# Products before the statistics: the first weight pair of three stages works on residual times channel scale

## The reference, cut to what matters

```python
def rms_norm(x, g):
    y = x32 * lax.rsqrt(jnp.mean(x32 * x32, axis=-1, keepdims=True) + RMS_EPS)
    return (y * g.astype(jnp.float32)).astype(x.dtype)
def modulate(h, shift, scale):
    return h * (1 + scale[:, None, :]) + shift[:, None, :]
...
    if layer == N_A_LAYERS:
        h_kv = modulate(rms_norm(x, kv_norm_g), kv_mod[:, 0], kv_mod[:, 1])
        kv_bands = shared_kv_bands(h_kv, kv_w, cos, sin)
    h = modulate(rms_norm(x, norm_g[layer, 0]), mod[:, 0, 0], mod[:, 0, 1])
    x = x + 0.5 * mod[:, 0, 2][:, None, :] * swiglu(h, ...)
    h = modulate(rms_norm(x, norm_g[layer, 1]), mod[:, 1, 0], mod[:, 1, 1])
    y = moba_mixer(h, ...) if layer < N_A_LAYERS else dilated_mixer(h, ...)
    x = x + mod[:, 1, 2][:, None, :] * y
    h = modulate(rms_norm(x, norm_g[layer, 2]), mod[:, 2, 0], mod[:, 2, 1])
    x = x + 0.5 * mod[:, 2, 2][:, None, :] * swiglu(h, ...)
```

## Time and profile before

| | us |
|---|---|
| median of 3 runs | 2489.45 |
| lowest, highest | 2488.74, 2490.04 |
| the profiled execution | 2490.71 |
| its span, first to last instruction | 2489.0 |
| mean granted TensorE clock | 0.997 |

### The profile page before, as it was taken

The page is one execution under the profiler, slowest core; times in us unless marked ns, Lnnn a source line. Parts: engine busy times, 40 slices in busy tenths (PEclk is TensorE's granted clock), DMA queues, the critical chain, the costliest instruction groups (busy, mean ns, idle before and its releaser), DMA issues. The chain is left out here.

```text
span 2489.0 us, 33283 instructions
## 1 busy us (share of the span) xinstructions
PE 2443.6 (98%) x11977; PEld 2015.8 (81%) x11985; DVE 1356.8 (55%) x2066; ACT 854.8 (34%) x1204; POOL 137.2 (6%) x128
## 2 busy tenths in 40 slices
PE   9999999999999999999999999999999999999998
PEld 6888886888778888878888888886888887888886
DVE  7555445677675654355545555445667667433333
ACT  3222223445443332233333333223344444333221
POOL 0000000112000000011211000000111110000000
PEclk9999999999999999999999999999999999999999
DMA  6666532665446654335557656345888973223332
GB/s 244 191 193 190 169 118 91 205 194 182 140 151 196 186 182 134 105 123 193 183 188 250 189 183 199 125 125 133 248 222 220 238 219 102 85 93 100 99 95 84
DMA packets 135714, 408.76 MB, mean 164 GB/s; under 512 B 17089, under 2 KB 17473, under 8 KB 135617
## 3 DMA queue, kind: packets, MB, share of 16 engines
q1 hardware_dynamic: 122560, 357.16, 47.6%
q0 software_dynamic: 13056, 50.33, 5.7%
HBM read 353.95 MB, written 52.43 MB: 163 GB/s over the span
## 5 line engine op out<-in xcount | busy, mean ns | idle before, releaser
L325 DVE TENSOR_TENSOR w_lo<-w_raw,w_hi 128x1024 fp32r<-128x1024 f32 (+2 forms) x386 | 473.3, 1227 | 650.5 <-ACT w_hi L321 650.5
L330 PE MATMUL ps<-h_hi,w_hi 128*128 128x512 f32 x1856 | 738.0, 398 | 11.0 <-DVE h_lo L880 4.6
L332 PE MATMUL ps<-h_hi,w_lo 128*128 128x512 f32 x1856 | 725.4, 391 | 0.0
L331 PE MATMUL ps<-h_lo,w_hi 128*128 128x512 f32 x1856 | 724.4, 390 | 0.0
L321 ACT CAST w_hi<-w_raw 128x1024 fp32r<-128x1024 f32 (+2 forms) x388 | 395.9, 1020 | 802.9 <-PE ps L332 788.2
L330 PEld LDWEIGHTS ps<-h_hi,w_hi 128*128 128x128 f32 x1856 | 349.6, 188 | 91.5 <-DVE h_lo L880 10.9
L332 PEld LDWEIGHTS ps<-h_hi,w_lo 128*128 128x128 f32 x1856 | 349.0, 188 | 74.2
L331 PEld LDWEIGHTS ps<-h_lo,w_hi 128*128 128x128 f32 x1856 | 349.9, 189 | 65.8
L330 PE MATMUL ps<-act_hi,w_hi 128*128 128x512 f32 x704 | 275.5, 391 | 0.0
L332 PE MATMUL ps<-act_hi,w_lo 128*128 128x512 f32 x704 | 274.2, 389 | 0.0
L331 PE MATMUL ps<-act_lo,w_hi 128*128 128x512 f32 x704 | 274.0, 389 | 0.0
(11 more groups left out here) (137 smaller groups left out, 2772.2 us busy)
## 6 DMA issues: line engine op xcount, KB each, us to landing
w_raw<-gate_up SPq DMA_DIRECT2D x176, 512.0 KB, 3.7
ada_raw<-ada SPq DMA_DIRECT2D x144, 512.0 KB, 4.6
w_raw<-down SPq DMA_DIRECT2D x80, 512.0 KB, 3.6
w_raw<-kv_w SPq DMA_DIRECT2D x48, 512.0 KB, 3.6
w_raw<-mixa_w SPq DMA_DIRECT2D x34, 512.0 KB, 4.3
w_raw<-mixb_w SPq DMA_DIRECT2D x34, 512.0 KB, 5.7
kb<-rot_st POOLq DMA_DIRECT2D x12, 1024.0 KB, 5.0
k_hi<-kb SPq DMA_DIRECT2D x64, 192.0 KB, 5.1
```

The costliest lines, as they stand in the source:

```text
L325: eng.tensor_tensor(w_lo[:, slot, 0:n], w_raw[:, slot, 0:n], w_hi[:, slot, 0:n].bitcast(F32), ALU.subtract).then_inc(w_lo_done[slot], 2)
L330: nc.tensor.matmul(out_ap, l_hi, r_hi, start=start, stop=False, skip_group_check=skip)
L331: nc.tensor.matmul(out_ap, l_hi, r_lo, start=False, stop=False, skip_group_check=skip)
L332: return nc.tensor.matmul(out_ap, l_lo, r_hi, start=False, stop=stop, skip_group_check=skip)
```

## The change

At the borders into mixA, kv and mixB, `pe_late_pair` takes the place of `pe_stats` and of the first weight pair. It multiplies the weights by x times channel scale, without token factor and shift. For the result h = x·a·r + s, with r a factor of the token and s a shift of the channel, the product of weights W and h is r·(W(x·a)) + W·s. So the two result banks are multiplied by r (`late_scale`, to SBUF), and W·s is summed by two-column products (`shift`: s as high and low column, with the high and the low weights) and added in `late_read`, together with the cosine or sine factor. The zero products of these borders are gone. Rows 0 to 5 of x times a (`late_high` on ACT, `late_low` on DVE) are made in the down projection after each of its first three pairs, rows 6 and 7 behind root and diagonal. The normalised h is still made row by row and is used from the second pair on; two weight splits stand in its midst (`LATE_SPLIT`). The stored modulation block moves behind the first reads, in kv TensorE's value products wait for it. The third weight transfer goes ahead of the tables on SP. In mixB the second pair takes its two units in an interleaved order, with bank 3 for its second.

The diff, cut to its core:

```diff
+LATE = ("mixA", "kv", "mixB")
+LATE_SPLIT = {"mixA": {1: 2, 5: 3}, "kv": {1: 2, 5: 3}, "mixB": {1: 2, 4: 3}}
+LATE_ROWS = (6, 7)
...
+        def pe_late_pair(pe, name):
+            e, r, u0, p0 = LATE.index(name), ROUND[name], UNIT0[name], PAIR0[name]
+            def weights(w, k, j):
+                if name == "mixB":
+                    return w[:, j, k * P:(k + 1) * P]
+                return w[:, k // 4, k % 4 * PAIR + j * P:k % 4 * PAIR + (j + 1) * P]
+            def rows(ks, halves=(0, 1)):
+                for k in ks:
+                    pe.wait_ge(late_lo_done, KT * e + k + 1)
+                    for j in halves:
+                        mm = three_passes(ps[:, j, :], weights(w_hi, k, j), weights(w_lo, k, j),
+                                          h_hi[:, k, :], h_lo[:, k, :], k == 0, k == KT - 1)
+                    if 1 in halves:
+                        mm.then_inc(late_used, 1)
+            def shift(ks, halves=(0, 1)):
+                for j in halves:
+                    for k in ks:
+                        for w in (w_hi, w_lo):
+                            mm = nc.tensor.matmul(shift_ps[:, 2 * j:2 * j + 2], weights(w, k, j), shift_hl[:, k, :],
+                                                  start=j == 0 and k == 0 and w is w_hi,
+                                                  stop=k == KT - 1 and w is w_lo, skip_group_check=True)
+                mm.then_inc(unit_used, 1)
+            def sums():
+                pe.wait_ge(sum_done, 9 * r)
+                for t in range(TT):
+                    mm = nc.tensor.matmul(stat[:, t:t + 1], tmp[:, 2, t * P:(t + 1) * P], ones[:, 0:1],
+                                          start=True, stop=True)
+                mm.then_inc(stat_done, 1)
+            def spread():
+                pe.wait_ge(diag_done, r + 1)
+                nc.tensor.matmul(rb, ones[:], diag[:].rearrange("p t n -> p (t n)"),
+                                 start=True, stop=True).then_inc(rb_done, 1)
+            pe.wait_ge(w_lo_done[0], u0 + 2)
+            pe.wait_ge(pair_free, p0 + 1)
+            pe.wait_ge(shift_split, 2 * e + 2)
+            if name == "mixB":
+                rows(range(4), (0,))
+                sums()
+                rows((4, 5), (0,))
+                pe.wait_ge(w_lo_done[1], u0 + 2)
+                rows((0, 1), (1,))
+                spread()
+                rows((6, 7), (0,))
+                shift(range(KT), (0,))
+                rows(range(2, KT), (1,))
+                shift(range(KT), (1,))
+            else:
+                rows((0, 1))
+                sums()
+                rows((2, 3))
+                spread()
+                shift(range(4))
+                pe.wait_ge(w_lo_done[1], u0 + 2)
+                rows(range(4, KT))
+                shift(range(4, KT))
+            pe.sem_inc(shift_summed, 1)
...
-            pe.wait_ge(pair_free, p0 + 2)
-            with pe.Fori(0, G * NB // 2) as i:
-                pe_pair(pe, i * 8 + u0, i * 4 + p0 - 2, 0, FULL_KS, kv_h_hi, kv_h_lo, h_ready)
-                pe_pair(pe, i * 8 + u0 + 2, i * 4 + p0 - 1, 2, FULL_KS, kv_h_hi, kv_h_lo)
+            def values(i):
                 for j in range(4):
                     pe.wait_ge(w_lo_done[j % 2], i * 8 + u0 + 4 + j - j % 2 + 2)
                     if j == 0:
-                        pe.wait_ge(rb_kept_done, 1)
+                        pe.wait_ge(rb_kept_done, LATE.index("kv") + 1)
+                        pe.wait_ge(xar_done, KT * NORMS.index("ffn2"))
                         pe.wait_ge(pair_free, i * 4 + p0 + 2)
...
+            pe.wait_ge(pair_free, p0 + 2)
+            pe_pair(pe, u0 + 2, p0 - 1, 2, FULL_KS, kv_h_hi, kv_h_lo, h_ready)
+            pe.wait_ge(shift_done, LATE.index("kv") + 1)
+            pe.wait_ge(mod_ready, ADA_IN_FFN[1] + ADA_LOOPED + 1)
+            values(0)
+            with pe.Fori(1, G * NB // 2) as i:
+                pe_pair(pe, i * 8 + u0, i * 4 + p0 - 2, 0, FULL_KS, kv_h_hi, kv_h_lo)
+                pe_pair(pe, i * 8 + u0 + 2, i * 4 + p0 - 1, 2, FULL_KS, kv_h_hi, kv_h_lo)
+                values(i)
...
-                    for n in range(24):
+                    for n in range(KT, 2 * KT) if is_a else (8, 9, 12, 13, 10, 11, 14, 15):
                         substep(g, n)
+                    for n in range(2 * KT, 24):
+                        substep(g, n)
+                    pe.wait_ge(shift_done, LATE.index(name) + 1)
...
+        def late_cols(dve, name, block, gain_row, col_n):
+            e = LATE.index(name)
             dve.wait_ge(mod_ready, block + 2)
             nc.vector.scalar_tensor_tensor(out=a_col[:], in0=mod[:, block + 1, :], scalar=1.0,
                                            in1=gain[:, gain_row, :], op0=ALU.add,
                                            op1=ALU.mult).then_inc(col_ready, 1)
+            if e > 0:
+                dve.wait_ge(shift_summed, e)
+            nc.vector.tensor_copy(shift_hl[:, :, 0], mod[:, block, :]).then_inc(shift_split, 1)
+            dve.wait_ge(shift_split, 2 * e + 1)
+            nc.vector.tensor_tensor(shift_hl[:, :, 1], mod[:, block, :], shift_hl[:, :, 0].bitcast(F32),
+                                    ALU.subtract).then_inc(shift_split, 1)
+            dve.wait_ge(col_ready, col_n)
+        def late_high(act, name, n, col_n):
+            act.wait_ge(col_ready, col_n)
+            nc.scalar.activation(h_hi[:, n, :], x[:, n, :], ACT.Copy, scale=a_col[:, n:n + 1]).then_inc(late_hi_done, 1)
+        def late_low(dve, name, n):
+            dve.wait_ge(late_hi_done, KT * LATE.index(name) + n + 1)
+            nc.vector.scalar_tensor_tensor(out=h_lo[:, n, :], in0=x[:, n, :], scalar=a_col[:, n:n + 1],
+                                           in1=h_hi[:, n, :].bitcast(F32), op0=ALU.mult,
+                                           op1=ALU.subtract).then_inc(late_lo_done, 1)
+        def late_views(name):
+            if name == "kv":
+                return rb_kept[:], next_tmp[:]
+            return att[:, 0, :], att[:, 1:3, :]
+        def late_scale(dve, name):
+            e, (factor, scaled) = LATE.index(name), late_views(name)
+            dve.wait_ge(shift_summed, e + 1)
+            nc.vector.tensor_reduce(shift_out[:], shift_ps.rearrange("p (j h) -> p j h", j=2),
+                                    mybir.AxisListType.X, ALU.add).then_inc(shift_done, 1)
+            dve.wait_ge(unit_used, UNIT0[name] + 2)
+            dve.wait_ge(rb_kept_done, e + 1)
+            view = by_class if name == "mixA" else classes
+            for j in range(2):
+                nc.vector.tensor_tensor(view(scaled[:, j, :]), classes(ps[:, j, :]), classes(factor),
+                                        ALU.mult).then_inc(late_scaled, 1)
+            dve.wait_ge(late_scaled, 2 * e + 2)
+            dve.sem_inc(pair_free, 1)
+        def late_read(dve, name, rope_n, half):
+            e, scaled = LATE.index(name), late_views(name)[1]
+            if half == 0:
+                dve.wait_ge(shift_done, e + 1)
+                dve.wait_ge(rope_done, rope_n)
+            for n in (2 * half, 2 * half + 1):
+                src, table = ((0, cos), (1, sin), (1, cos), (0, sin))[n]
+                op = nc.vector.scalar_tensor_tensor(out=tmp[:, n, :], in0=scaled[:, src, :],
+                                                    scalar=shift_out[:, src:src + 1], in1=table[:],
+                                                    op0=ALU.add, op1=ALU.mult)
+            op.then_inc(late_rope, 1)
...
+                if name in LATE and k - 1 in LATE_SPLIT[name]:
+                    n = LATE_SPLIT[name][k - 1]
+                    w_split_lo(dve, UNIT0[name] + n, n % 2)
             low(KT - 1)
+            if name in LATE:
+                late_scale(dve, name)
...
+                if name in LATE and name != "kv":
+                    act.wait_ge(late_used, KT * LATE.index(name) + k + 1)
                 nc.scalar.activation(view(to_hi[:, k, :]), classes(tmp[:, 3 + k % 2, :]), ACT.Identity,
                                      bias=mod[:, block, k:k + 1]).then_inc(h_hi_done, 1)
+                if name in LATE and k in LATE_SPLIT[name]:
+                    n = LATE_SPLIT[name][k]
+                    w_split_hi(act, UNIT0[name] + n, n % 2)
+            if name in LATE:
+                act.wait_ge(xar_done, x0 + KT)
+                nc.scalar.copy(late_views(name)[0], rb).then_inc(rb_kept_done, 1)
+                w_split_hi(act, UNIT0[name] + 4, 0)
...
+                    if late is not None:
+                        for j in range(2):
+                            if i * 4 + 2 * b + j not in LATE_ROWS:
+                                late_high(act, late[0], i * 4 + 2 * b + j, late[1])
...
+                    w_split_lo(dve, u0 + 4, 0)
+                    mod_store(dve, ADA_IN_FFN[1] + ADA_LOOPED)
+                    for half in range(2):
+                        late_read(dve, "kv", 2 * n0, half)
+                    w_split_lo(dve, u0 + 5, 1)
```

(23 more changed lines are left out.)

146 lines of the change are left out of this document (90 added, 56 removed).

## The result

The changed kernel takes 2503.97 us (median of 4 runs, 2503.59 to 2507.19) where the kernel before, beside it, takes 2489.66. The ratio is 1.0061, 95% interval 1.0043 to 1.0078. It is **slower by 14 us**; 11 us faster was forecast. The profiled execution took 2503.81, span 2502.1 (before 2490.71 and 2489.0).

The account below looks back on a forecast made before the run. TensorE, busy for 98% of the span, was taken as the bound, with empty work at three borders. Gains 2.5 + 4.1 + 6.0 less 1.7 made 10.9 us: forecast 2478.5, range 2472 to 2485.

Parts of the forecast that it names:

- What is moved at no cost: Down projection and borders: late rows, norm rows, third weight transfer and POOL's additions were said to move without cost.
- 0.23: TensorE's pitch in us for a 512-column product in full flow, used to size the first pair's 48 products at 11.0.
- The slower rival: Late rows in the down projection push a split past its unit; nine pairs lose 2.8 each: 2503.8, chance 0.05.
- What would show it: Signs at the borders: first part 16.6, two-column products 0.115, mixA waits 2.4 and about 3, unit 7 six us earlier.
- kv, 4.1: Border into kv: second pair begins at 1088.8 instead of 1092.91, no wait behind it, gain 4.1 us.
- mixA, 2.5: Border into mixA: VectorE's chain to the keys limits the gain to 2.5 us, between 1 and 4.9.
- The wait before it: MixA, unit 4: TensorE waits 2.4 us for VectorE's weight split, done at 435.9.
- the 1.7 of the sum: One clock fall, expected from the 3.1 us idle before mixA's first score, costing 1.7 us.
- The clock's rival: The clock falls at the narrow sums too: 13.6 against 12.6, so 2490.4, no change; chance 0.09.
- mixB, 6.0: Border into mixB: unit 7's weight transfer comes 6 us earlier, gain 6.0 us, between 2.4 and 7.
- The first rival: The first queries' store may hold unit 7's transfer; mixB gives 2.4, 7.3 in all, 2482.1; chance 0.14.

Follow-up runs that it names:

- e7: The changed kernel with its idle tile 96 bytes shorter, so the streamed tiles stand where they stood in the kernel before: 2484.36 us, ratio 0.9979.
- e5: The changed kernel with unused columns in shift_out, so tiles behind it stand 256 bytes further on than in the kernel before: 2483.96 us, ratio 0.9978.
- e8: The changed kernel with tiles placed as in e7 and mixB's key load issued after unit 5, not right ahead of unit 7: 2480.38 us, ratio 0.9960.
- e12: The same kernel as e8 once more, over more rounds, beside the kernel before: 2481.53 us, ratio 0.9966.
- e4: The kernel before with act_lo alone moved by 32 bytes: 2501.12 us, ratio 1.0034.
- e2: The kernel before with an unused tile of 32 bytes per partition ahead of the tile idle: 2512.18 us, ratio 1.0090.
- e10: The kernel before with an unused tile of 32 bytes between h_lo and w_raw: 2518.33 us, ratio 1.0114.
- e6: The kernel before with an unused tile of 32 bytes ahead of x, moving all large tiles together: 2489.99 us, ratio 1.0006.

## Why the prediction was wrong

- **The failed step** is one that the working doesn't have. "What is moved at no cost" follows the instructions that the change moves, and not the tiles. Two new small tiles shift the streamed tiles by 96 bytes against the weights, and 20.2 us of the 25 between forecast and result are that (e7: 19.6 back). "0.23" was taken as the pitch of a full-flow product without asking what it depends on; 0.228 becoming 0.234 hardly shows in two digits, but it stands for some 3200 products.
- **The slower rival** had the sign and nearly the figure (2503.8), with a mechanism that did not occur: no product waits in the late rows' stretches, and the down projections are longer by their pitch alone.
- **What would show it**: the signs named for the first parts, for mixA and for kv came (16.3 to 16.4 against 16.6, 0.11 against 0.115, the waits of 2.13 and 3.39, none at kv, the clock at 1.00); unit 7 of mixB six us earlier did not come (1.4). They said nothing of the 20 us, since each looked at a border.
- **kv, 4.1**: measured 4.3 to 4.5. **mixA, 2.5**: 2.3 up to the first score. The wait before it came at 2.4 by a slip: the working's own 422.0 + 11.0 is 433.0, not 433.5, which would make it 2.9; measured 2.13. The clock fell behind the wait for keys as forecast (granted 0.79 from 460 to 468, 1.7 us), yet over the whole stretch 2.1 remain after, 1.3 in e7 and 2.2 in e5; so less of the fall came through than the 1.7 of the sum.
- **The clock's rival** fell: granted 1.00 stands over all first parts, narrow sums and shift sums included. The earlier trace rows were weak evidence for what waits do: of the two falls shown, one came after 1.43 us of idling and 0.9 of narrow products, the other after 2.15 of narrow products without idling. The waits of 3.39 and 5.14 in the changed kernel are the ones that a fall follows.
- **mixB, 6.0**, is the mis-sized term: 0.8 measured in the changed kernel, 0.9 in e5, 1.2 lost in e7. The chain to unit 7 was taken to be the weight transfer's, seen in the earlier trace rows. That transfer did come early: it landed 41.9 us after the border's start, 48.4 before, so 6.5 sooner. What the working left out is what would then come last: ScalarE's split stood behind the rotation that waited for the store. The first rival named the store of the first queries, and the figure 2.4, but had it hold the transfer, which it did not; it was put aside with "the key load is issued by a split". That it is was the trouble: the key load moved up 5.1 with its split (6 were forecast), the store only 1.4, since the half reads, the block and the rotation stand ahead of it. All the keys came to stand ahead of the store. e8 shows it by one move: 4 us of time, the wait and the clock's fall gone.
- With both repaired (e8) the borders give 1.4, 4.3 and 5.9: 11.5 us of stretches, against 10.9 forecast; its repeat e12 gives 1.0, 4.3 and 3.7: 9.0. In time 2480.38 is 9.5 below the kernel before, and e12 has 8.8. This is the fastest of the kernels run here. That it comes near the forecast is in part luck, since the key load was moved besides.

Open: how much a product loses at which distance. 32, 96 and 128 bytes gave 123.0 to 123.6 for a down projection, 64 gave 121.1 to 121.7, 0 and 256 gave 120.1 to 120.5; other distances weren't tried. In e4 one of the two products that stream the unmoved act_hi was slowed, the one that stands ahead of act_lo's, so whether a product is hindered by its own weights' place or by the load or stream next to it isn't settled. Why the place matters inside TensorE's reads isn't shown either.

## What to carry to other kernels

A new tile, however small, moves all that are allocated behind it. List the places of the large tiles before and after, keep the distance between what TensorE streams and where its weights lie (here at a multiple of 256 bytes), and declare small tiles last or pad them. In a comparison of two traces, take the same products' first and last start in stages that the change doesn't touch before explaining those it does. When steps move by different amounts, look for pairs whose order turns, above all a load that comes to stand ahead of a store for which an engine waits.

## What the runs showed of the hardware

- The pitch of a 128x512 product in full flow depends on the place of the streamed tile against the weight tile: 120.1 to 120.5 us for 528 products where both stand alike modulo 256 bytes, 121.1 to 121.7 at a distance of 64, up to 123.6 at 32, 96 and 128. 32 unused bytes made this kernel slower by 21 us (e2) or, between other tiles, by 28 (e10), and by nothing where all tiles moved together (e6). No wait and no lower clock goes with it, and it is there with all other engines and transfers at rest (0.2267 and 0.2333 us for the last 28 products).
- A store is slowed by loads of another queue: the same store, issued at the same point, freed its tile after 12.1 us when eight key loads had been issued 1.9 to 5.2 us ahead of it (e7), and after 7.1 and 8.6 when they had been issued 11 to 14 us ahead (e8, e12).
